# In-projection, attention and linear attention of a first block, merged into one stream of steps

## The reference

```python
h = rmsnorm(x, norm1_w)
proj = h @ w_in                                   # 1024 -> q, k, v of 6+6 heads, q, k, v, r, gate of 4 linear heads
y_a = dilated_attention(aq, ak, av, bias_a)       # 6 heads, softmax, causal, relative bias
y_b = gla(bq, bk, bv, br, ba, ...)                # 4 heads, chunked gated linear attention, chunks of 16 tokens
y_c = moba_attention(cq, ck, cv, bias_c)          # 6 heads, softmax, causal, relative bias
x = x + concatenate([y_a, y_b, y_c]) @ w_out
x = x + square(relu(rmsnorm(x) @ w_ff1)) @ w_ff2
```

## Time and profile before

| what | value |
|---|---|
| time, median of 3 runs | 2698.64 us (2695.71 to 2701.97) |
| profiled execution, its own time | 2698.94 us |
| its span | 2697.1 us |
| PE busy | 2450.9 us (91%) |
| DVE, ACT, POOL busy | 1342.9 (50%), 912.2 (34%), 603.7 us (22%) |
| HBM traffic | 86 GB/s over the span |

### The profile page before, as it was taken

One profiled execution on the slowest core, in us unless ns is written; L12 is line 12 of the kernel. 1 busy time (PEld: TensorE's weight loads), 2 busy tenths in 40 slices (PEclk: granted clock), 3 DMA queues, 4 the chain that ended last, 5 costly groups with the idle time before them and its releaser, 6 DMA issues.

```text
span 2697.1 us, 28260 instructions
## 1 busy us (share of the span) xinstructions
PE 2450.9 (91%) x10858; PEld 1826.1 (68%) x10858; DVE 1342.9 (50%) x2091; ACT 912.2 (34%) x1471; POOL 603.7 (22%) x552
## 2 busy tenths in 40 slices
PE   5998757999999899898989999999899898999998
PEld 4763235777777686444678888888767445788886
DVE  4235544687885745534344444444454544443434
ACT  5225433322223321355344222222232454422222
POOL 1210121333332122100223222222031102222221
PEclk9997868999999899999889999999999999899999
DMA  5520002466663132101113333332132111232321
GB/s 171 160 79 28 32 0 63 135 196 192 189 197 102 32 101 81 32 24 32 32 47 109 103 95 112 102 96 89 36 99 75 34 32 47 78 96 92 98 90 55
DMA packets 70770, 233.46 MB, mean 87 GB/s; under 512 B 8624, under 2 KB 11809, under 8 KB 70637
## 3 DMA queue, kind: packets, MB, share of 16 engines
q1 hardware_dynamic: 49328, 165.04, 19.6%
q0 software_dynamic: 18256, 63.48, 7.9%
q10 hardware_dynamic: 3052, 3.13, 0.4%
HBM read 223.73 MB, written 7.90 MB: 86 GB/s over the span
## 4 chain that ended last, share of the span: by engine, by line
PE 74%; DVE 12%; ACT 5%; issue 5%; POOL 4%; DMA 0%; ACTq 0%; DVEq 0%; POOLq 0%
PE psum L504 35%; PE psum L737 18%; DVE mod_scratch L1214 4%; PE psum L1065 4%; PE psum L1036 3%; PE psum L561 2%; PE psum L993 2%; PE psum L638 1%; PE psum L1051 1%; POOL weight_split L2533 1%; POOL hidden_tmp L2688 1%; DVE residual L1505 1%; PE psum L475 1%; PE psum L462 1%; PE psum L666 1%
## 5 line engine op out<-in xcount | busy, mean ns | idle before, releaser
L504 PE MATMUL psum<-mix_split,weight_split 128*128 128x512 f32 (+1 forms) x3840 | 805.7, 371 | 31.4 <-DVE mix_split L1461 12.8
L504 PEld LDWEIGHTS psum<-mix_split,weight_split 128*128 128x128 f32 x3840 | 664.4, 191 | 174.5 <-issue 27.6
L737 PE MATMUL psum<-hidden,weight_split 128*128 128x512 f32 (+1 forms) x3072 | 636.7, 367 | 11.7 <-DVE residual L1505 5.9
L737 PEld LDWEIGHTS psum<-hidden,weight_split 128*128 128x128 f32 x3072 | 524.2, 188 | 120.9 <-POOL weight_split L2533 8.2
L1951 ACT CAST weight_split<-weight_ring 128x1024 fp32r<-128x1024 f32 x269 | 276.5, 1041 | 305.4 <-PE psum L737 288.3
L2533 POOL TENSOR_TENSOR weight_split<-weight_ring,weight_split 128x1024 fp32r<-128x1024 f32 x89 | 224.8, 2526 | 423.1 <-ACT weight_split L1951 422.3
L1490 DVE TENSOR_TENSOR hidden<-hidden_tmp,hidden 128x512 fp32r<-128x512 f32 (+1 forms) x128 | 138.2, 1099 | 355.6 <-POOL hidden_tmp L2688 355.6
L1128 DVE TENSOR_TENSOR weight_split<-weight_ring,weight_split 128x1024 fp32r<-128x1024 f32 x180 | 233.0, 1297 | 42.9 <-ACT weight_split L1951 42.8
L2228 ACT ACTIVATE hidden_tmp<-psum 128x512 f32<-128x512 f32 (+1 forms) x128 | 69.0, 539 | 524.2 <-PE psum L504 512.9
L504 PE MATMUL psum<-normed_in,weight_split 128*128 128x512 f32 (+1 forms) x1080 | 217.4, 362 | 9.4 <-DVE normed_in L1182 6.9
L1507 DVE SCALAR_TENSOR_TENSOR residual<-psum,modulation,residual 128x512 f32<-128x512 f32 x192 | 120.8, 658 | 191.5 <-PE psum L737 191.5
(11 more groups left out here) (295 smaller groups left out, 2394.1 us busy)
## 6 DMA issues: line engine op xcount, KB each, us to landing
weight_ring<-in_w_mlp SPq DMA_DIRECT2D x128, 512.0 KB, 3.6
weight_ring<-in_w_ff SPq DMA_DIRECT2D x64, 512.0 KB, 4.3
mod_ring<-in_w_mod POOLq DMA_DIRECT2D x64, 512.0 KB, 4.0
weight_ring<-in_w_in SPq DMA_DIRECT2D x45, 512.0 KB, 4.1
squares<-in_w_mod POOLq DMA_DIRECT2D x64, 256.0 KB, 3.2
weight_ring<-in_w_out SPq DMA_DIRECT2D x24, 512.0 KB, 3.6
weight_ring<-in_tables SPq DMA_DIRECT2D x13, 512.0 KB, 3.7
weight_ring<-in_w_v SPq DMA_DIRECT2D x8, 512.0 KB, 4.3
```

The lines of the kernel that those rows point to most:

```text
L504: m = pe.matmul(psum[:, b + r, 0:hi - lo], w[:, part_w, :], x[:, part_x, k, lo:hi], start=k == 0 and part_w + part_x == 0, stop=k == KT - ...
L737: mm = pe.matmul(psum[:, b + r, 0:hi - lo], w[:, part_w, :], G[:, part_x, f % (2 * GROUP), lo:hi], start=jj == 0 and part_w + part_x == 0, ...
```

## The change

Stages 1 to 3 become one function, `mixers()`, in each engine's program. Its parts are:

- **Order of the tiles.** `IN1` lists the 17 tiles anew: the gate input (16), linear q (6) and k (7) first; then all 8 value slices, with the linear heads' values in the first half; then the first attention pair's q and k tiles 0 and 3, and tile 1. Six tiles stand before attention; the other 11 are "between" tiles, each cut in 8 steps of 3 matmuls.
- **Half ticks.** A counter `at` runs in all engines. Four half ticks follow the first two tiles, two follow each further tile or value slice (for a tile, PE has them after its 4th and 8th slice, the other engines both after `keep`), and two belong to each of the 52 attention ticks (n = -4 to 47), so half tick 28 begins attention and 131 is the last. In each half tick, `strips_at(h)` and `linear_at(h)` emit what is due at h: strips at h = 7 to 18, the gate at h = 4 to 10, transposed values at 14 and 16, the 32 pair products (s, two each) at h = 18 to 49, the chunk sums and states at h = 50 to 71, the carried states at 73 to 91, the roots at 96, the output gate at 117 to 120, and the mix splits at 119 on.
- **PE in an attention tick**: logits of step n+4, turned of step n, values every fourth tick, then twice: a linear half tick and 3 projection matmuls. The between tiles end with tick 43; the last 8 ticks have none.
- **One bank for the linear part.** All linear products use PSUM bank 7, so each waits until DVE or ACT has read the one before.
- **Buffers.** Queries and keys are kept for two pairs of heads only; POOL multiplies the decays in place, first by q, then by k, after the Exp. Attention probabilities have one buffer per i.
- **States.** The scan, the copies to blocks and the memsets go; DVE carries the state by 32 dependent operations of 64 columns that read the chunk sums in PSUM. Each state then meets q per head: 124 products of 16 columns and 64 output rows, 248 instructions, where there were 124.
- **Output gate.** Exp on ACT, then plus one and `reciprocal` on DVE (512 columns), where ACT took Exp, Ln, Exp.
- **Condition vectors.** silu is computed once, on 128 partitions x 16 columns, stored to DRAM by a POOL DMA, and read back as a broadcast where it is used; the silu steps of the late modulation go. ACT issues four input loads (three constants of the strips, the condition) before its first squares; three of these stood after the norm. The broadcast loads are issued by POOL just before the first modulation load.
- **SP** loads strips as before, with the weight loads of the between tiles issued ahead of each.

The core of the diff, with the new functions of PE; the other engines' follow the same order:

```diff
+        IN1 = [16, 6, 7, 0, 3, 1, 4, 2, 5, 10, 13, 11, 14, 12, 15, 8, 9]
+        BEFORE = 6
+        PAIRS = [(0, 3), (1, 4), (2, 5), (10, 13), (11, 14), (12, 15)]
+        LEAD = 4
...
+        GATE, VT, PAIR, KTOK, U_AT, CARRY, ROOTS, LAST_GATE, SPLIT_MIX = 4, 14, 18, 50, 52, 73, 96, 117, 119
...
+            def linear_at(h):
+
+                b = 7
...
+                if PAIR <= h < PAIR + 2 * B_CHUNK:
+                    s, pr = divmod(h - PAIR, 2)
+                    n = NCHUNK * (B_CHUNK - s)
+                    wait_bank(b)
+                    pe.wait_ge(*when("gla_pool", ("qk_decay", s)))
+                    m = pe.matmul(bank(b, n), C["spread"][64 * pr:64 * pr + 64, :], gla["decays"][64 * pr:64 * pr + 64, s % 2, 0:n],
+                                  start=True, stop=True)
+                    m.then_inc(*did("gla_pe", ("pairs", s, pr)))
+                    freed[b] = [("gla_vec", ("times_v", s, pr))]
...
+                    for n in range(max(1, 4 * part), 4 * part + 4):
+                        for hd in (2 * pr, 2 * pr + 1):
+                            r0 = 64 * (hd % 2)
+                            m = pe.matmul(psum[r0:r0 + DH, b, n * B_CHUNK:(n + 1) * B_CHUNK], gla["state"][32 * hd:32 * hd + 32, n - 1, :],
+                                          gla["eb"][32 * hd:32 * hd + 32, n * B_CHUNK:(n + 1) * B_CHUNK], start=True, stop=True)
...
+                def alone(i):
+                    for k, _ in enumerate(project(i)):
+                        if k % 4 == 3:
+                            half_tick()
+                alone(IN1[2])
+                for half, banks in enumerate(((0, 1, 2, 5), (6, 0, 1, 2))):
+                    for _ in project_values(half, banks):
+                        half_tick()
+                        half_tick()
+                for i in IN1[3:BEFORE]:
+                    alone(i)
+                between = (k for i in IN1[BEFORE:] for k in project(i))
+                for n in range(-LEAD, len(ATT)):
+                    if n + LEAD < len(ATT):
+                        logits(n + LEAD)
+                    if n >= 0:
+                        turned(n)
+                        if n and n % 4 == 0:
+                            values(n // 4 - 1)
+                    for _ in range(2):
+                        half_tick()
+                        next(between, None)
```

and of DVE and POOL in `linear_at`:

```diff
+                if u_taken(h) is not None:
+                    t = u_taken(h)
+                    ve.wait_ge(*when("gla_pe", ("u", 4 * t + 3)))
+                    for n in range(8 * t, 8 * t + 8):
...
+                        ve.wait_ge(*when("gla_vec", ("state", n - 1)))
+                        ve.scalar_tensor_tensor(out=ST_[:, n, :], in0=ST_[:, n - 1, :], scalar=gla["dec"][:, n:n + 1], in1=u, op0=ALU.mult,
+                                                op1=ALU.add).then_inc(*did("gla_vec", ("state", n)))
...
+                if h in (LAST_GATE, LAST_GATE + 1):
+                    pr = h - LAST_GATE
+                    x = (la, kt)[pr]
+                    ve.wait_ge(*when("gla_act", ("gate_exp", pr)))
+                    ve.tensor_scalar(x[:, :], x[:, :], 1.0, None, ALU.add).then_inc(*did("gla_vec", ("gate_one", pr)))
+                    ve.wait_ge(*when("gla_vec", ("gate_one", pr)))
+                    ve.reciprocal(x[:, :], x[:, :]).then_inc(*did("gla_vec", ("gate_inverse", pr)))
...
+                    po.wait_ge(*when("gla_act", ("decay", s)))
+                    po.tensor_tensor(x, x, ch(B_[:, 0, :])[:, :, s:], ALU.mult).then_inc(*did("gla_pool", ("q_decay", s)))
+                    po.wait_ge(*when("gla_pool", ("q_decay", s)))
+                    po.tensor_tensor(x, x, ch(B_[:, 1, :])[:, :, 0:w], ALU.mult).then_inc(*did("gla_pool", ("qk_decay", s)))
```

More of the change, by code:

```diff
@@ L247, in build @@
[L247 to L255, removed]
@@ new lines, in project @@
+            def project(i):
+                b = take(1, "gemm")
+                bank_of["in1", i] = b
+                j = split_at[use_load("w_in1", i, split=True)]
+                pe.wait_ge(*when(lo_of(j), j))
+                wait_bank(b)
+                for k in range(KT):
+                    w = WS[:, j % SPLIT_RING, :, k * P:(k + 1) * P]
+                    for part_w, part_x in ((0, 0), (0, 1), (1, 0)):
+                        m = pe.matmul(bank(b), w[:, part_w, :], HS_1[:, part_x, k, :], start=k == 0 and part_w + part_x == 0, stop=k == KT - 1 and part_w == 1)
+                    if k == KT - 1:
+                        m.then_inc(*did("gemm", ("in1", i)))
+                    yield
+                split_use[j] = ("in1", i)
+                freed[b] = [in1_keep(i)]
@@ new lines, in logits @@
+            def logits(n):
+                u, i = ATT[n]
+                b = take(1, "row")
+                bank_of["att", "logits", n] = b
+                wait_bank(b)
+                if n % 8 == 0:
+                    for tile in PAIRS[u // 2]:
+                        pe.wait_ge(*when(*in1_keep(tile)))
+                r0, p = 64 * (u % 2), u // 2
+                m = pe.matmul(psum[:, b, 0:(i + 1) * P], QK[r0:r0 + DH, p % 2, 0, i * P:(i + 1) * P], QK[r0:r0 + DH, p % 2, 1, 0:(i + 1) * P],
+                              start=True, stop=True)
+                m.then_inc(*did("att_pe", ("logits", n)))
+                freed[b] = [("att_vec", ("bias", n))]
@@ new lines, in mixers @@
+                        if s == 3:
+                            ac.wait_ge(*when("gemm", ("v1", half, 3)))
+                            for t in (0, 2):
+                                ac.copy(V[:, t, half * 512:(half + 1) * 512], bank(bank_of["v1", half, t])).then_inc(*did("in1_act", ("v", half, t)))
+                        half_tick()
+                        half_tick()
+                for i in IN1[3:BEFORE]:
+                    stage("w_in1", i)
+                    keep(i)
+                    half_tick()
+                    half_tick()
```

1257 lines of the change are left out of this document (597 added, 660 removed).

## The result

The changed kernel takes **2680.69 us** (median of five, 2672.24 to 2683.74), the kernel before it on the same chip 2698.64 us. The ratio is 0.9925, 95% interval 0.9904 to 0.9947: faster, but by under 1%, 18 us where 59 were forecast. That is 17 us above the range that the forecast gave for itself (2615 to 2664) and 2.7 us above the one that takes in its nearer rivals (2595 to 2678). The profiled execution took 2682.28 us, its span is 2680.4 us.

A forecast was written before the change was run, and what follows sets the result against it. No single engine bounds attention or linear attention; work is chained across engines, so PE's one list at full clock plus handovers was priced. 2698.9 - 55.2 (out-projection at 366) - 5 + 1.5 = 2640 us; range 2615 to 2664.

The forecast's parts named there:

- its nearer rivals: Alternative outcomes inside 2595 to 2678 us, a range leaving out the slower case and the tails of two others.
- the clock: PE's granted clock in the merged attention ticks: 1.0 expected nearly throughout, with 4 us added for stretches where it is not.
- Ticks 0 to 10: Attention ticks with pair products: PE and DVE both near 3.2 us per tick, waiting through one bank; 43 us.
- The 2 us kept for it: Pair stage: allowance for DVE operations with two SBUF inputs waiting on POOL; 23 us if applied every time, about 2 kept.
- Ticks 11 to 21: Attention ticks with chunk sums: PE's 49 us plus four waits of about 1.5 us for DVE's states; 55 us.
- Ticks 22 to 33: Attention ticks with carried states: 248 instructions at 0.07 us on PE's path, 2 us of handovers; 59 us.
- Ticks 34 to 43: Attention ticks with projection left: PE 31.5 us, plus ACT's table loads and roots later than its slack; 36 us.
- Ticks 44 to the out-projection: Last eight ticks, no projection left: DVE's 25.6 us, with two reciprocals at 4.1 us each; 29 us with handovers.
- Up to attention: Everything before the first attention logits: PE's work of 128.8 us plus 11 us of stalls, so attention starts at 140.
- Behind the out-projection: Rest of the kernel: -5 us from the late silu gone, +1.5 us for the first modulation product's broadcast loads.
- Rival 2: Attention ticks: a PE-DVE rendezvous in every half tick leaves no slack; mean tick 5.0, 2674 us; chance 0.13.
- Rival 3: Attention ticks: single bank puts product, read and release in series; tick 5.8, deciding from 5.5 on; 2716 us, chance 0.05.

The follow-up runs named there:

- run 8: The kernel before the change, with only its pair products padded to all 128 rows by zero weights: 2703.79 us, ratio 1.0022.
- Run 1: Changed kernel with all pair products run over all 128 rows, zero weights in the half not meant: 2639.81 us, ratio 0.9779.
- run 3: Changed kernel without the pair work of distances 5 to 15 on all engines (output incomplete): 2632.81 us, one run.
- run 2: Changed kernel with both linear half ticks of a tick first, then six projection matmuls together: 2654.28 us, ratio 0.9846.
- Runs 4 and 5: Changed kernel, one edit each: 4 replaced the output gate's reciprocals by multiplications, 2662.89 us; 5 moved all low parts of the mixes to POOL, 2666.03 us.
- run 9: Changed kernel with pair products over 128 rows, all mix low parts on POOL, output gates at half ticks 110 and 117: 2635.08 us, ratio 0.9769.

## Why the prediction was wrong

**The step that failed is the clock**: "it sank in the old stages where PE waited; I expect 1.0 nearly throughout, and 4 us". The rows behind it were right as readings (0.82 and 0.62 in stages where PE was busy 84% and 49% of the time), the reason drawn from them was not the only one. One row of before would have warned: in its last stage PE was busy without a gap for 13.9 us on 64-row products and had 0.50 (run 8). In the changed kernel PE was busy 97% of ticks 0 to 10 and had 0.56. Run 1 adds no work to PE's list and gives it more waits, and returns 1.00 and 30 us; run 3 takes the pair products out and finds 1.00 too. Shown is that the pair products on 64 of 128 rows, each two instructions ahead of a group of three matmuls, held the clock at 1.2 GHz there; grouped otherwise (run 2) they did so only in part. Run 8 shows that padded pair products alone do not bring the clock back in the old stage, in which PE waits in one part and works on other 64-row products in another. Not separated is what about a product on 64 rows counts: the rows that stay unused, or the weight load behind it that is not covered (below). The padding changes both, as the timelines of run 1 show. Not tried either is to issue the two products of a distance side by side in two banks, as the kernel before does.

In this case a PE busy 97% of 76 us was granted 0.56, and one busy 87% of 46 us (40.2 us) 1.00. The Trainium skill, "TensorE: Matmul & The Clock Gate", section "Part 1: The HAM clock gate", lets the clock follow from how busy PE has been. Taken with the busy share of the trace, that rule gives the opposite order of these two; the measurement decides, and here it was the padding of the products that made the difference.

By the terms, measured less forecast:

- **Ticks 0 to 10, +33.1.** 30.1 is what the padding returned (76.1 less run 1's 46.0): the clock, and with it the shorter way from a pair product through its group, 0.1 to 0.4 us each at full clock, which was not priced apart. The other 3.0 is left at full clock, where the chain runs through DVE: 37.7 us busy instead of 35.5. The addition of 352 columns took 0.774 beside POOL's multiplications and 0.524 before:

```profile
L1392 DVE TENSOR_TENSOR gla_acc<-gla_acc,gla_mul 128x352 f32<-128x352 f32 x2 | 1.5, 774 | 0.1
...
L1389 DVE TENSOR_TENSOR gla_mul<-psum,gla_vT 128x352 f32<-128x352 f32 x2 | 1.0, 520 | 0.2 <-PE psum L680 0.2
...
L1378 DVE TENSOR_TENSOR gla_decays<-gla_b 128x160 f32<-128x160 f32 x1 | 2.1, 2097 | 0.0
```

  These are of run 1. The product, which has one input in PSUM, kept its 0.52; the addition, both of whose inputs are in SBUF, did not, and one gap of 160 columns waited through POOL's weight split (2.37 us; the gap of 192 columns took 0.34). This is the rule of the Trainium skill, "SBUF — State Buffer", section "SBUF: two separate sides", that the prediction weighed: present in run 1, at some 4 us (the additions of 384 to 96 columns and that gap, against their lengths before), not at 23. The 2 us kept for it were half of it. In the changed kernel, with the clock at 1.2 GHz, such waits were hidden: PE was later than DVE.
- **Ticks 11 to 21, +8.6.** I took 0.70 for three projection matmuls from a row where 24 follow one another. Behind a linear product they take 0.90 at full clock, and a pair of chunk-sum products 0.97 instead of 0.83: 22 x 0.20 + 16 x 0.15 = 6.8. The waits for DVE's states are 4.0 in two places, of 6 forecast. The rest, 3.8, goes with the clock, 0.91: after the longer of these waits, 3.1 us, the three matmuls of the next group take 1.58 us.
- **Ticks 22 to 33, -6.0.** Carried states cost 0.57/16 = 0.036 each, not 0.07: 248 of them 8.4 us less. Some 16 groups with an uncovered load give back 16 x 0.20 = 3.2, and PE waits 1.3 us where 2 were kept for handovers. Chain of waits, tick 24:

```profile
288.72 0.57 PE psum L709 x16
289.29 0.90 PE psum L628 x3
```

- **Ticks 34 to 43, -2.8.** PE was busy 31.3 us, as summed, and waited 1.9; the table loads and roots were covered by ACT's slack but for that.
- **Ticks 44 to the out-projection, +10.8.** The forecast summed DVE's work (25.6; measured 21.65, a reciprocal being 3.35 and not 4.1) and added 3.4 for handovers. But PE's only cover was gone, so each of DVE's extras stood in front of a softmax step and PE waited through it. DVE's groups there:

```profile
L1438 DVE RECIPROCAL gla_kt<-gla_kt 128x512 f32<-128x512 f32 x1 | 3.4, 3354 | 0.0
...
L1449 DVE TENSOR_TENSOR mix_split<-residual,mix_split 128x512 fp32r<-128x512 f32 x2 | 3.1, 1542 | 2.0 <-ACT mix_split L2137 2.0
...
L1449 DVE TENSOR_TENSOR mix_split<-gla_mix,mix_split 128x512 fp32r<-128x512 f32 x1 | 1.3, 1339 | 1.4 <-ACT mix_split L2137 1.4
```

  Runs 4 and 5 price them at 5.7 and 6.7 us, one edit at a time. Those eight ticks are a chain through three engines, and I had costed them as the sum of one.

These five are 43.7; less the 4 that the clock had been given, 39.7, and with the 2.5 us by which attention started late 42.2, as the out-projection shows.

**What held.** Up to attention: 142.5 against 140, with DVE's product the largest wait of PE (5.0 us in 3 waits) and 0.6 for a raw strip, none for POOL; runs 1, 5 and 9 began at 138.0, 138.8 and 136.1. Behind the out-projection -3.7 against -3.5, closer than can be told: the same code took 2263 to 2272 us there in the runs above, so the agreement to 0.2 us is luck, and of its two terms, -5 and +1.5, neither was measured by itself. The late silu is gone, PE works through it; the first modulation product waits for its loads and stands at 488.25. Timeline of DVE:

```profile
488.25 1.23 DVE L1305 CUSTOM_DVE_ANT_0 mod_scratch<-mod_ring,cond 128x1024 f32<-128x1024 f32 x1 [2.19 <-DMA mod_ring<-in_w_mod]
```

The structure of the forecast (how long each stage takes once the clock is there) is what run 9 shows: 46.0, 59.6, 53.0, 37.2, 30.6 against 43, 55, 59, 36, 29. With the clock and the last eight ticks mended, the merge gives 2631 to 2635 us. As it stands it gives 18 us.

**The rivals.** Rival 2 gave the nearest time (2674, mean tick 5.0; measured 265.7/52 = 5.1, past the 5 that the prediction named as its own refutation), by another mechanism: PE waits for a partner mainly in the last eight ticks (19.3 of 39.8 us), not in every half tick. Rival 3's point, a mean of 5.5, was passed in ticks 0 to 10 (6.9 each), again by the clock and not by handovers. None of the four named a low clock on a busy PE, and the range, bounded by stalls alone, missed by what that was worth.

## What to carry to other kernels

Read the granted clock beside the kind of matmul, not beside PE's idle time alone: before work that fills only part of the rows is spread between full products, ask what clock a busy PE had on such work (here 0.50, in a stretch of 14 us), and bound it at the lower level (here 30 us). Where such products must be mixed in, filling the rows with zero weights costs no instruction and can return more than the merge itself. Look first whether two of them run side by side on different rows: there padding makes them pass in turn (10 us more of PE here). And when filler work runs out before the chain that it covers, cost the end as a chain with everything that shares a list with it, and put the extras where the filler still is.

## What the runs showed of the hardware

- Granted clock 0.56 with PE busy 97%, 1.00 with the same instructions on 128 rows and PE busy 87%. Lengthening the groups of full products from three to six matmuls, with the 64-row products kept, gave 0.85. With products of 64 rows alone, PE busy 13.9 of 13.9 us had 0.50.
- Two float32 products on rows 0 to 63 and 64 to 127, issued one behind the other, pass side by side: 2.17 us for two of 512 columns at clock 0.50, against 3.75 for the same two on all rows.
- Three 512-column matmuls behind a pair product, a chunk sum or a carried state take 0.90 us, in a row of 24 they take 0.70, both at full clock. Six behind a pair product take 1.59 in run 2, so the 0.20 is paid once per group. Behind transposes, which fill rows and columns, six take 1.40.
- Instructions of 16 columns on 32 rows and 64 output rows pass at 0.036 us each when 16 stand in a row at full clock; with 128 output rows and a lower clock it was 0.112. Which of the two made the difference was not tried.
- A DVE reciprocal of 512 columns takes 3.35 us and one of 1 column 0.15: 6.3 ns a column, near the 7.8 of the narrow ones and far from that of other operations (a multiplication of 512 columns takes 0.63 to 0.67).
- DVE's additions with two SBUF inputs stretch beside POOL's multiplications, in the mean of two by half at 352 columns (0.52 to 0.77, run 1) and to twice at 224 (0.39 to 0.78, changed kernel); its products from PSUM do not (0.52 and 0.39 in the same places).
